# Products of 768 columns taken as two passes of 384 columns, with context and latents in one tensor

## The chip, the cores and the metric

The kernel runs on one core of a Trainium2 chip. The metric is the device time of one execution in microseconds, and the median of several runs stands for a kernel. "Columns" below are the columns of a matmul's moving operand, one per token.

## The reference, cut to what matters

Two transformer blocks run one after the other, each of two layers. The first block has 256 context tokens beside 512 latent tokens, 768 in all, and in its first layer (and in the keys and values of its second) both take part; after that only the 512 latents go on. The stretch that the change touches is this:

```python
hx = rms_norm(x, norm1_g[0]) * (1 + mod_x[1]) + mod_x[0]        # 512 latents
hc = rms_norm(s_c, norm1_g[0]) * (1 + mod_c[1]) + mod_c[0]      # 256 context tokens
y_c, y_x = hybrid_mixer(hc, hx, hyb_w_in[0], ...)               # h @ w_in, mLSTM heads, short conv, @ w_out
x = x + mod_x[2] * y_x
x = x + mod_x[5] * sqrelu_mlp(norm2(x), mlp_w1[0], mlp_w2[0])
s_c = s_c + mod_c[2] * y_c
s_c = s_c + mod_c[5] * sqrelu_mlp(norm2(s_c), mlp_w1[0], mlp_w2[0])
```

The same weights multiply the context and the latents, so one product covers 768 columns. `sqrelu_mlp` is `square(relu(h @ w1)) @ w2` with 4096 hidden channels.

## The kernel before, in words

Channels lie on the 128 partitions and tokens along the free dimension, context first (columns 0 to 255) and latents after (256 to 767). A *tile* is one weight block of 1024 by 128: it gives 128 output channels for all tokens. Weights arrive by DMA into one of four slots (`Wraw`); ScalarE writes the rounded upper part `Whi` (L1391) and VectorE the rest `Wlo` (L2038). Activations are likewise kept as a pair, `hi` and `lo`. For each of the eight 128-channel steps `k` TensorE issues three matmuls, `Whi` by `hi`, `Whi` by `lo` and `Wlo` by `hi`, each with its own weight load, all adding into the tile's accumulator. Tile `t` uses the accumulator `G[t % 2]`, two PSUM banks of 512 columns; `ps(bank, a, b)` places columns 0 to 255 in the upper half of the first bank and 256 to 767 in the whole second bank.

A product over all tokens is a FULL product; `parts(FULL)` is `[(0, 256), (256, 768)]`. The lines the text speaks of:

- `product` (L648 to L650): all eight `k` for the context columns, then all eight for the latents. So 24 matmuls of 256 columns follow each other, then 24 of 512.
- `first_products` (L675 to L677): the two first tiles of a group, interleaved over `k` because their source is still being made; three matmuls of 256 and three of 512 alternate.
- `full_part` (L827 to L829), called by `full_end` and `full_start`: the *joints*, where a layer ends with a residual and a norm and the next one begins. There the two parts are apart on purpose, since the context's norm is worked out while the latents still multiply. Two tiles end a joint and three begin the next.

The 768-column stretch is, in order: the hybrid layer's input tiles (25, the first two by another path), its output tiles (8: two by `first_products`, four by `product`, two by `full_end`), and the MLP (64 tiles in four chunks of 8 tiles up and 8 tiles down, the first three of chunk 0 by `full_start`, the last two of chunk 3 by `full_end`). The order on every engine is written out by hand, and each engine waits on semaphores.

The tensors that hold a layer's input (`h0`, `h1`) and the MLP's hidden activations (`hid0`) each come as four pieces, context and latents apart (`wide`, class `Wide`), with small spacers named `..._line` that set where a tensor begins. In the MLP, ScalarE takes a tile out of `G` with a ReLU (L1514), VectorE squares it (L2238), ScalarE writes the upper part `hid hi` in two pieces (L1518) and VectorE the rest in two pieces (L2243). In the first joint ScalarE writes the upper part of the normed input (L1473, function `upper`), VectorE the rest (L2161). Memory of finished stages is used again: the sources of the hybrid layer's output product (`mixa`, `mixb`, `mixc`) share their place with later tensors.

Of the kernel before, what the change touches and what calls it, by code (L numbers as in the profile page):

```python
# [7 lines left out]
ALU = mybir.AluOpType  # L8
# [102 lines left out]

class WideRow:
# [16 lines left out]
def build(nc, xin, cvec, wstream, adaw, firstw, vecs_d, consts_d, rope_d, poolw_d, sguw_d, rows_d, out):  # L129
    ctx = ExitStack()  # L130
    with ctx:
# [7 lines left out]
        def wide(name, ctx_line, lat_line, where, lat_first):  # L139

            half = {}
            for part, n, at in (("lat", NX, lat_line), ("ctx", NC, ctx_line))[::1 if lat_first else -1]:
                if at:
                    sb(f"{name}_{part}_line", [P, at], where=where)
                half[part] = [sb(f"{name}_{part}_{x}", [P, KD, n], F32R, where) for x in ("hi", "lo")]
            return [Wide(half["ctx"][i], half["lat"][i]) for i in range(2)]

# [81 lines left out]
        h0 = wide("h0", 16, 16, p1, False)  # L229
        p1.close()  # L230
        p2 = ExitStack()
        sb("mixa_line", [P, 112], where=p2)
# [7 lines left out]
        h1 = wide("h1", 48, 48, p4, True)  # L240
        hid0 = wide("hid0", 0, 16, p4, False)
# [95 lines left out]


# [4 lines left out]
        rep_ready, pick_ready, rstd_kept, ctx_shifted = map(sem, ("rep_ready", "pick_ready", "rstd_kept", "ctx_shifted"))  # L343
# [24 lines left out]
        chi_ready, upper_ready = map(sem, ("chi_ready", "upper_ready"))  # L368
# [22 lines left out]
        def parts(rng):  # L391
            return [(0, NC), (NC, NT)] if rng == FULL else [(NC, NT)]

# [240 lines left out]
        def _(pe):  # L634
            def product(t, src, rng, kt=KD, from_group=False):

                wait(pe, w_lo, t + 1)
                wait(pe, tile_free[t % 2], t // 2 + (-1 if from_group else 0))
                s = t % 4
                for a, b in parts(rng):  # L640
                    for k in range(kt):
                        hi, lo = src(k)
                        if is_apart(t):
                            wh, wl = [w[:, k * P:(k + 1) * P] for w in w_of(t)[1:]]
                        else:
                            wh, wl = Whi[:, s, k * P:(k + 1) * P], Wlo[:, s, k * P:(k + 1) * P]
                        o = ps(G[t % 2], a, b)
                        pe.matmul(o, wh, hi[:, a:b], start=(k == 0), stop=False)  # L648
                        pe.matmul(o, wh, lo[:, a:b], start=False, stop=False)  # L649
                        last = pe.matmul(o, wl, hi[:, a:b], start=False, stop=(k == kt - 1))  # L650
                last.then_inc(tile_done, 1)

            def first_products(t, src, rng, sem, at, kt=KD, between=None, order=None, lag=None):


                lag = lag or (3 if rng == FULL else 4)
                for n in range(kt + lag):
                    if between is not None:
                        between(n)
                    for e, nth in ((0, n), (1, n - lag)):  # L660
                        if not 0 <= nth < kt:
                            continue
                        k = order[nth] if order else nth
                        u = t + e
                        s = u % 4
                        if nth == 0:
                            wait(pe, w_lo, u + 1)
                            wait(pe, tile_free[u % 2], u // 2)
                        if e == 0:
                            pe.wait_ge(sem, (at + (nth + 1)).value())  # L670
                        hi, lo = src(k)
                        wh, wl = Whi[:, s, k * P:(k + 1) * P], Wlo[:, s, k * P:(k + 1) * P]
                        for a, b in parts(rng):
                            o = ps(G[u % 2], a, b)
# [34 lines left out]
            def first_column(i):  # L709

                pe.wait_ge(row_kept, i + 1)
                if i == 0:
                    pe.wait_ge(pick_ready, 1)
# [134 lines left out]
            def full_end(f, t0, src):  # L848

                for p in range(2):  # L850
                    for j in range(2):
# [4 lines left out]
                        for k in range(KD):  # L856
                            last = full_part(t, src, p, k, k == 0, k == KD - 1)
                            if p == 1 and j == 0 and k == 3:
                                full_stats(f, 0)
                        last.then_inc((f_a_done, tile_done)[p], 1)  # L860
# [524 lines left out]
        def _(act):  # L1385
# [74 lines left out]
            def full_edge(f, t0):  # L1460
# [41 lines left out]
            def mlp(t0, hid, rng, h0_, after, edge=None):  # L1502
# [3 lines left out]
                def chunk(i, c0, last=False):  # L1506
                    for j in range(CH):
# [4 lines left out]
                        g = e_tile(t, j) if group else ps(B6 if third else G[t % 2], a0, b0)  # L1512
# [3 lines left out]
                        for a, b in parts(rng):  # L1516
# [243 lines left out]
            for t in range(N_HYB):  # L1760
# [8 lines left out]
                g = ps(G[t % 2], a, b)  # L1769
# [256 lines left out]
        def _(dve):  # L2026
# [81 lines left out]
            def add_residual(t, m, rng, par, gate):  # L2108

                evac(t)  # L2110
                for a, b in parts(rng):
                    v = 1 if a == 0 else 0
                    last = dve.scalar_tensor_tensor(out=X[:, m, a:b], in0=ps(G[t % 2], a, b),  # L2113
# [91 lines left out]
            def mlp(t0, hid, rng, h0_, par, ada_layer, ada_par, vectors, before, after):  # L2205
# [3 lines left out]
                def chunk(i, c0, last=False):  # L2209
# [21 lines left out]
                    for j in range(CH):  # L2231
# [9 lines left out]
                        for a, b in parts(rng):  # L2241
                            hi, lo = [x.part(j, a, b) if rng == FULL else x[:, j, a - off:b - off] for x in hid]
                            last_lo = dve.tensor_tensor(lo, SQ[:, j % 2, a:b], hi.bitcast(F32), ALU.subtract)  # L2243
                        last_lo.then_inc(hid_ready, 1)
# [270 lines left out]
            for k in range(KD):  # L2515
# [3 lines left out]
                              ALU.add).then_inc(pick_ready, 1)  # L2519
# [191 lines left out]
            for t in range(N_HYB):  # L2711
                if t not in (2, 4):
                    split_lo(At(t + 2))
                g = G[t % 2]
# [23 lines left out]
                if 9 <= t < 17 and t % 2 == 0:  # L2738
# [7 lines left out]
                    dve.tensor_tensor(T[:, 0, 1:1 + NC], SQ[:, j % 2, 0:NC], ps(g, 0, NC), ALU.mult)  # L2746
                    link(dve.tensor_tensor(T[:, 0, 3 + NC:3 + NT], SQ[:, j % 2, NC:NT], ps(g, NC, NT), ALU.mult))
# [7 lines left out]
                if 17 <= t < 21:  # L2755
                    j = t - 17
                    dve.wait_ge(tile_done, t + 1)
                    dve.tensor_tensor(CY[:, j, 1:1 + NC], CY[:, j, 1:1 + NC], ps(g, 0, NC), ALU.mult)
                    link(dve.tensor_tensor(CY[:, j, 3 + NC:3 + NT], CY[:, j, 3 + NC:3 + NT], ps(g, NC, NT), ALU.mult))
# [545 lines left out]
```

## Time and profile before

| | |
|---|---|
| median of 3 runs | 2515.29 us (2514.77 to 2516.95) |
| profiled execution, first to last instruction | 2512.5 us; it is listed with no time of its own beside this span |
| TensorE busy | 2491.2 us, 99% of the span, 14058 matmuls |
| VectorE, ScalarE busy | 1611.4 us (64%), 972.5 us (39%) |
| TensorE's granted clock | mean 0.998 of full speed |
| chain that ended last | TensorE 96% |

How to read it: a row of the time line gives the start, the length, the engine, the line and the operands. Matmuls are pipelined and their ends are modelled, so the length of a matmul's row is longer than the time it costs. What a matmul costs is the distance from its start to the next one's start.

### The profile page before, as it was taken

The page shows a single profiled execution, that of the slowest core. Times are in us where ns is not written, and L with a number is a line of the kernel's source. Part 1 is how long each engine was busy: PE and PEld are TensorE (multiplying, and loading weights), DVE is VectorE, ACT ScalarE, POOL GpSimd, SP SyncE. Part 2 cuts the span into 40 slices and gives each one's busy share as a digit, 9 for nine tenths or more (in the row PEclk, how much of TensorE's full clock was granted, in tenths as well). Part 3 has the DMA queues.
Part 4 walks back from the last instruction along what each step waited for, and adds up shares of the span by engine and source line. Part 5 has one row for each costly group of instructions (what it writes and reads, how often), then busy time and mean ns, then how long its engine had stood idle before and what let it go on. Part 6 is the DMA issues. An engine that isn't in the chain of part 4 may idle for free.

```text
span 2512.5 us, 36307 instructions
## 1 busy us (share of the span) xinstructions
PE 2491.2 (99%) x14058; PEld 2125.8 (85%) x14058; DVE 1611.4 (64%) x2551; ACT 972.5 (39%) x1483; POOL 117.9 (5%) x211
## 2 busy tenths in 40 slices
PE   8999999999999999999999999999999999999998
PEld 6888888888888888779888888898888888888887
DVE  5777667665546567766655575776667777644446
ACT  6243533131313245764332244353232454533224
POOL 0000000100000000000000000010001000000000
PEclk9999999999999999999999999999999999999999
DMA  7323314433333321002545553224546323132222
GB/s 288 120 99 110 127 50 143 159 118 110 114 110 134 110 76 51 2 1 93 199 152 169 173 192 113 101 88 172 187 158 219 135 95 110 68 101 93 100 96 97
DMA packets 83965, 303.70 MB, mean 121 GB/s; under 512 B 9200, under 2 KB 11376, under 8 KB 83568
## 3 DMA queue, kind: packets, MB, share of 16 engines
q1 hardware_dynamic: 58336, 208.92, 24.0%
q0 software_dynamic: 25488, 92.81, 10.8%
q8 instruction: 100, 1.64, 0.3%
q14 instruction: 41, 0.34, 0.0%
HBM read 299.60 MB, written 2.10 MB: 120 GB/s over the span
## 4 chain that ended last, share of the span: by engine, by line
PE 96%; DMA 2%; DVE 1%; issue 0%; ACT 0%; SPq 0%; POOL 0%; POOLq 0%; ACTq 0%; DVEq 0%
PE G L648 20%; PE G L650 20%; PE G L649 20%; PE G L675 5%; PE G L676 5%; PE G L677 5%; PE G L742 2%; PE G L743 2%; PE G L744 2%; PE B L1243 2%; PE G L827 1%; DMA Araw<-adaw_dram 1%; PE G L829 1%; PE G L828 1%; PE B L1219 1%; PE G L1203 1%
## 5 line engine op out<-in xcount | busy, mean ns | idle before, releaser
L1391 ACT ACTIVATE Whi<-Wraw 128x1024 fp32r<-128x1024 f32 x333 | 349.6, 1051 | 411.4 <-DMA Wraw<-wstream_dram 399.3
L2038 DVE TENSOR_TENSOR Wlo<-Wraw,Whi 128x1024 fp32r<-128x1024 f32 x333 | 406.9, 1222 | 116.4 <-ACT Whi L1391 115.2
L648 PE MATMUL G<-hs_hi,Whi 128*128 128x512 f32 x672 | 264.2, 393 | 0.0
L650 PE MATMUL G<-hs_hi,Wlo 128*128 128x512 f32 x672 | 261.6, 389 | 0.0
L649 PE MATMUL G<-hs_lo,Whi 128*128 128x512 f32 x672 | 261.5, 389 | 0.0
L2053 DVE SCALAR_TENSOR_TENSOR Araw<-Araw,CB 128x1024 f32<-128x1024 f32 x176 | 214.3, 1220 | 20.6 <-DMA Araw<-adaw_dram 20.5
L2113 DVE SCALAR_TENSOR_TENSOR X<-G,MOD,X 128x256 f32<-128x256 f32 (+1 forms) x104 | 65.2, 655 | 206.0 <-PE G L650 154.9
L594 POOL DMA_DIRECT2D Araw<-adaw_dram x176 | 93.2, 530 | 1692.4 <-DVE Araw L2053 1637.9
L648 PE MATMUL G<-h_lat_hi,Whi 128*128 128x512 f32 x424 | 165.7, 391 | 0.0
L649 PE MATMUL G<-h_lat_lo,Whi 128*128 128x512 f32 x424 | 165.1, 389 | 0.0
L650 PE MATMUL G<-h_lat_hi,Wlo 128*128 128x512 f32 x424 | 165.1, 389 | 0.0
L648 PE MATMUL G<-hid_hi,Whi 128*128 128x512 f32 x408 | 158.9, 389 | 0.7 <-DVE X L3160 0.7
L650 PE MATMUL G<-hid_hi,Wlo 128*128 128x512 f32 x408 | 158.7, 389 | 0.0
L649 PE MATMUL G<-hid_lo,Whi 128*128 128x512 f32 x408 | 158.7, 389 | 0.0
L648 PEld LDWEIGHTS G<-hs_hi,Whi 128*128 128x128 f32 x672 | 126.2, 188 | 27.3 <-issue 1.7
L649 PEld LDWEIGHTS G<-hs_lo,Whi 128*128 128x128 f32 x672 | 126.2, 188 | 26.6 <-issue 1.0
L650 PEld LDWEIGHTS G<-hs_hi,Wlo 128*128 128x128 f32 x672 | 126.2, 188 | 26.4
L1514 ACT ACTIVATE T<-G 128x768 f32<-128x768 f32 (+1 forms) x61 | 43.0, 704 | 205.4 <-PE G L650 122.2
L2238 DVE TENSOR_TENSOR SQ<-T 128x768 f32<-128x768 f32 (+1 forms) x64 | 52.7, 823 | 87.7 <-ACT T L1514 87.7
L648 PE MATMUL G<-h_ctx_hi,Whi 128*128 128x256 f32 x368 | 104.8, 285 | 0.3 <-ACT T L1514 0.3
L649 PE MATMUL G<-h_ctx_lo,Whi 128*128 128x256 f32 x368 | 103.0, 280 | 0.0
L650 PE MATMUL G<-h_ctx_hi,Wlo 128*128 128x256 f32 x368 | 102.9, 280 | 0.0
(636 smaller groups left out, 6169.5 us busy)
## 6 DMA issues: line engine op xcount, KB each, us to landing
Wraw<-wstream_dram SPq DMA_DIRECT2D x333, 512.0 KB, 3.3
Araw<-adaw_dram POOLq DMA_DIRECT2D x176, 512.0 KB, 3.8
Eraw<-wstream_dram SPq DMA_DIRECT2D x22, 512.0 KB, 4.4
FIRST<-firstw_dram SPq DMA_DIRECT2D x6, 1024.0 KB, 18.7
X<-xin_dram SPq DMA_DIRECT2D x4, 768.0 KB, 7.0
X<-xin_dram SPq DMA_DIRECT2D x2, 1536.0 KB, 7.3
out_dram<-X SPq DMA_DIRECT2D x16, 128.0 KB, 1.7
ROW<-rows_dram SPq DMA_DIRECT2D x2, 768.0 KB, 6.5
```

The lines of the kernel that those rows point to most:

```text
L594: pool.dma_start(Araw[:, n % 2, :], adaw[bass.ds(n.value(), 1), :, :].rearrange("a p n -> p (a n)") if n.i is not None else adaw[n.c]).the ...
L648: pe.matmul(o, wh, hi[:, a:b], start=(k == 0), stop=False)
L649: pe.matmul(o, wh, lo[:, a:b], start=False, stop=False)
L650: last = pe.matmul(o, wl, hi[:, a:b], start=False, stop=(k == kt - 1))
L675: pe.matmul(o, wh, hi[:, a:b], start=(nth == 0), stop=False)
L676: pe.matmul(o, wh, lo[:, a:b], start=False, stop=False)
L677: last = pe.matmul(o, wl, hi[:, a:b], start=False, stop=(nth == kt - 1))
L1391: act.activation(hi, raw, ACT.Copy).then_inc(w_hi, 1)
L2038: dve.tensor_tensor(lo, raw, hi.bitcast(F32), ALU.subtract).then_inc(w_lo, 1)
L2053: last = dve.scalar_tensor_tensor(out=products, in0=Araw[:, n % 2, :], scalar=1.0, in1=CB[:, v, :], op0=ALU.mult, op1=ALU.mult, accum_out=o)
L2113: last = dve.scalar_tensor_tensor(out=X[:, m, a:b], in0=ps(G[t % 2], a, b), scalar=MOD[:, par, v, gate * 8 + m:gate * 8 + m + 1], in1=X[:, ...
L2238: dve.tensor_tensor(SQ[:, j % 2, a0:b0], T[:, j % 2, a0:b0], T[:, j % 2, a0:b0], ALU.mult).then_inc(hsq2_ready, 1)
```

## The change

FULL products outside the joints are taken as `(0, 384)` and `(384, 768)`. `even` says which tiles; `wide_at` places their 768 columns in the middle of the accumulator's 1024, so that each half lies in one bank.

```diff
+class Whole:
+    def part(self, k, a, b):
+        return self.ap[:, k, a:b]
...
+        def even(t):
+            c = t.c
+            if 2 <= c < T_HOUT + N_OUT - 2:
+                return True
+            return T_MLP0 + 3 <= c < T_ATT - 2
+        def wide_at(t, a, b):
+            return G[t % 2][:, P + a:P + b] if even(t) else ps(G[t % 2], a, b)
...
+        HALF = NT // 2
+        def halves(t, rng):
+            if rng == FULL and even(t):
+                return [(0, HALF), (HALF, NT)]
+            return parts(rng)
...
                 s = t % 4
-                for a, b in parts(rng):
+                for a, b in halves(t, rng):
                     for k in range(kt):
...
-                        o = ps(G[t % 2], a, b)
+                        o = wide_at(t, a, b) if rng == FULL else ps(G[t % 2], a, b)
```

A half of 384 columns crosses the border between context and latents, so the source must be one tensor. `h0`, `h1` and `hid0` become one tensor of 768 columns each (`whole`, class `Whole`); the spacer ahead of `mixa` shrinks from 112 to 32 numbers. Readers of `G` (L1514, L2113, the hybrid layer's) take `wide_at`. The hidden activations are written in one piece:

```diff
-                        for a, b in parts(rng):
-                            hi = hid[0].part(j, a, b) if rng == FULL else hid[0][:, j, a - off:b - off]
-                            last_hi = act.activation(hi, SQ[:, j % 2, a:b], ACT.Copy)
-                        last_hi.then_inc(hidhi_ready, 1)
+                        hi = hid[0].part(j, a0, b0) if rng == FULL else hid[0][:, j, a0 - off:b0 - off]
+                        act.activation(hi, SQ[:, j % 2, a0:b0], ACT.Copy).then_inc(hidhi_ready, 1)
```

The context part of the new `h1` now lies where `mixc` lay, and ScalarE writes it while the last output tile still multiplies. So that tile takes its `mixc` steps first, and ScalarE's first write waits for them (the semaphore `pick_ready` is merged into `rep_ready` to make room for `conv_used`):

```diff
-                        for k in range(KD):
-                            last = full_part(t, src, p, k, k == 0, k == KD - 1)
+                        order = HOUT_K if f == 0 and p == 1 and j == 1 else range(KD)
+                        for n, k in enumerate(order):
+                            last = full_part(t, src, p, k, n == 0, n == KD - 1)
...
+                            if f == 0 and p == 1 and j == 1 and n == 1:
+                                last.then_inc(conv_used, 1)
...
                 def upper(p, k):
+                    if f == 0 and p == 0 and k == 0:
+                        act.wait_ge(conv_used, 1)
                     act.wait_ge(f_t, 16 * f + 8 * p + k + 1)
```

On TensorE, inside the hybrid layer's input tiles, the end of one tile and the start of the next read before as follows (`h_ctx`, `h_lat` are the two pieces of the source; between the tiles stand products of the mLSTM heads):

```order
L648 MATMUL G<-h_lat_hi,Whi 128x512
L649 MATMUL G<-h_lat_lo,Whi 128x512
L650 MATMUL G<-h_lat_hi,Wlo 128x512
L1051 MATMUL B<-RM_hi,PICK 128x256
...
L648 MATMUL G<-h_ctx_hi,Whi 128x256
L649 MATMUL G<-h_ctx_lo,Whi 128x256
L650 MATMUL G<-h_ctx_hi,Wlo 128x256
```

and now:

```order
L685 MATMUL G<-h_hi,Whi 128x384
L686 MATMUL G<-h_lo,Whi 128x384
L687 MATMUL G<-h_hi,Wlo 128x384
L1091 MATMUL B<-RM_hi,PICK 128x256
...
L685 MATMUL G<-h_hi,Whi 128x384
L686 MATMUL G<-h_lo,Whi 128x384
L687 MATMUL G<-h_hi,Wlo 128x384
```

The number of matmuls and of weight loads and their places in the order stay; only the columns of each are 384 and 384 where they were 256 and 512.

On TensorE at the last tile of the first joint, second part, before:

```order
L844 MATMUL B<-CON,small 128x128
L827 MATMUL G<-mixa_hi,Whi 128x512
L828 MATMUL G<-mixa_lo,Whi 128x512
L829 MATMUL G<-mixa_hi,Wlo 128x512
```

and now, with `mixc` first:

```order
L881 MATMUL B<-CON,small 128x128
L864 MATMUL G<-mixc_hi,Whi 128x512
L865 MATMUL G<-mixc_lo,Whi 128x512
L866 MATMUL G<-mixc_hi,Wlo 128x512
L864 MATMUL G<-mixc_hi,Whi 128x512
L865 MATMUL G<-mixc_lo,Whi 128x512
L866 MATMUL G<-mixc_hi,Wlo 128x512
```

The `mixc` steps stood fourth and fifth of the tile's eight and stand first and second; the mark for ScalarE is on the sixth matmul of the tile.

On ScalarE from that joint into the MLP (with the semaphores waited for), before:

```order
L1473 ACTIVATE h_ctx_hi<-T,MOD 128x256 [waits f_t] x6
L1391 ACTIVATE Whi<-Wraw 128x1024 [waits tile_done,w_raw3]
...
L1514 ACTIVATE T<-G 128x768 [waits tile_done]
L1518 ACTIVATE hid_ctx_hi<-SQ 128x256 [waits hsq2_ready]
L1518 ACTIVATE hid_lat_hi<-SQ 128x512
L1514 ACTIVATE T<-G 128x768 [waits tile_done]
```

and now:

```order
L1515 ACTIVATE h_hi<-T,MOD 128x256 [waits f_t,conv_used]
L1515 ACTIVATE h_hi<-T,MOD 128x256 [waits f_t] x5
L1431 ACTIVATE Whi<-Wraw 128x1024 [waits tile_done,w_raw3]
...
L1557 ACTIVATE T<-G 128x768 [waits tile_done]
L1560 ACTIVATE hid_hi<-SQ 128x768 [waits hsq2_ready]
L1557 ACTIVATE T<-G 128x768 [waits tile_done]
```

The first write of the normed input has one more wait, and each hidden tile has one write where it had two; VectorE's L2243 is joined in the same way.

## Rows read from the trace of the kernel before

**Rows 1.** The page: span, busy times, TensorE's granted clock in 40 slices, the chain's shares

```profile
span 2512.5 us, 36307 instructions
...
PE 2491.2 (99%) x14058; PEld 2125.8 (85%) x14058; DVE 1611.4 (64%) x2551; ACT 972.5 (39%) x1483; POOL 117.9 (5%) x211
...
PEclk9999999999999999999999999999999999999999
...
PE 96%; DMA 2%; DVE 1%; issue 0%; ACT 0%; SPq 0%; POOL 0%; POOLq 0%; ACTq 0%; DVEq 0%
```

**Rows 2.** TensorE's waits: us in total, times, longest

```profile
PE G L751 <- DVE RS L2288: 1.5, 1, 1.5
...
PE G L648 <- ACT T L1514: 0.3, 1, 0.3
```

**Rows 3.** Time line of TensorE, MLP (start, length): 24 latent, then 24 context matmuls

```profile
410.12 0.39 PE L648 MATMUL G<-h_lat_hi,Whi 128*128 128x512 f32 x1
...
415.56 0.28 PE L648 MATMUL G<-h_ctx_hi,Whi 128*128 128x256 f32 x1
...
418.39 0.39 PE L648 MATMUL G<-h_lat_hi,Whi 128*128 128x512 f32 x1
```

**Rows 4.** Time line, a hybrid-layer tile: its second context matmul, its first latent one

```profile
245.81 0.28 PE L649 MATMUL G<-h_ctx_lo,Whi 128*128 128x256 f32 x1
...
248.42 0.39 PE L648 MATMUL G<-h_lat_hi,Whi 128*128 128x512 f32 x1
```

**Rows 5.** Time line of the context pass of rows 3, with weight loads (PEld)

```profile
415.80 0.28 PE L650 MATMUL G<-h_ctx_hi,Wlo 128*128 128x256 f32 x1
415.80 0.19 PEld L648 LDWEIGHTS G<-h_ctx_hi,Whi 128*128 128x128 f32 x1
...
415.92 0.28 PE L648 MATMUL G<-h_ctx_hi,Whi 128*128 128x256 f32 x1
```

**Rows 6.** Time line, second layer: eight matmuls of 2 columns with new weights each

```profile
964.22 0.95 PE L1161 MATMUL B<-CON,SQ 128*128 128x2 f32 x8
965.03 0.48 PE L648 MATMUL G<-h_lat_hi,Whi 128*128 128x512 f32 x1
```

**Rows 7.** TensorE by line and shape, 382 to 905 us (MLP): count, busy, mean ns

```profile
L649 PE MATMUL G<-h_lat_lo,Whi 128*128 128x512 f32 x184 | 71.6, 389 | 0.0
...
L649 PE MATMUL G<-h_ctx_lo,Whi 128*128 128x256 f32 x184 | 51.7, 281 | 0.0
...
L649 PE MATMUL G<-hid_ctx_lo,Whi 128*128 128x256 f32 x176 | 49.5, 281 | 0.0
...
L676 PE MATMUL G<-hid_ctx_lo,Whi 128*128 128x256 f32 x64 | 18.0, 281 | 0.0
...
L676 PE MATMUL G<-h_ctx_lo,Whi 128*128 128x256 f32 x48 | 13.5, 281 | 0.0
```

**Rows 8.** The same, 49 to 286.5 us (hybrid layer, input tiles)

```profile
L649 PE MATMUL G<-h_ctx_lo,Whi 128*128 128x256 f32 x184 | 51.3, 279 | 0.0
```

**Rows 9.** The same, 286.5 to 345 us (hybrid layer, output tiles): one latent, one context group

```profile
L648 PE MATMUL G<-mixa_hi,Whi 128*128 128x512 f32 x16 | 6.3, 395 | 0.0
...
L649 PE MATMUL G<-mixa_lo,Whi 128*128 128x256 f32 x16 | 4.5, 280 | 0.0
```

**Rows 10.** Time line, first joint: a matmul of the last output tile, ScalarE's first write

```profile
350.58 0.39 PE L829 MATMUL G<-mixa_hi,Wlo 128*128 128x512 f32 x1
...
351.75 0.91 ACT L1473 ACTIVATE h_ctx_hi<-T,MOD 128x256 fp32r<-128x256 f32 x2 [1.15 <-DVE T L2154]
```

**Rows 11.** Time line, start of the MLP: ScalarE writes a hidden tile, takes the next out

```profile
380.71 0.42 ACT L1518 ACTIVATE hid_ctx_hi<-SQ 128x256 fp32r<-128x256 f32 x1 [1.03 <-DVE SQ L2238]
381.03 0.61 ACT L1518 ACTIVATE hid_lat_hi<-SQ 128x512 fp32r<-128x512 f32 x1
381.55 0.79 ACT L1514 ACTIVATE T<-G 128x768 f32<-128x768 f32 x1
```

More of the change, by code:

```diff
@@ L109, in row, with __init__ @@
         return WideRow(self, k)
+class Whole:
+    def __init__(self, ap):
+        self.ap = ap
+    def part(self, k, a, b):
+        return self.ap[:, k, a:b]
+    def row(self, k):
+        return WideRow(self, k)
 class WideRow:
@@ L146, in wide, with whole @@
             return [Wide(half["ctx"][i], half["lat"][i]) for i in range(2)]
+        def whole(name, at, where):
+            if at:
+                sb(f"{name}_line", [P, at], where=where)
+            return [Whole(sb(f"{name}_{x}", [P, KD, NT], F32R, where)) for x in ("hi", "lo")]
         def sem(name):
@@ L228, in build @@
         p1 = ExitStack()
-        h0 = wide("h0", 16, 16, p1, False)
+        h0 = whole("h0", 32, p1)
         p1.close()
         p2 = ExitStack()
-        sb("mixa_line", [P, 112], where=p2)
+        sb("mixa_line", [P, 32], where=p2)
         mixa = [sb("mixa_hi", [P, 4, NT], F32R, p2), sb("mixa_lo", [P, 4, NT], F32R, p2)]
@@ L239, in build @@
         p4 = ExitStack()
-        h1 = wide("h1", 48, 48, p4, True)
-        hid0 = wide("hid0", 0, 16, p4, False)
+        h1 = whole("h1", 48, p4)
+        hid0 = whole("hid0", 128, p4)
         p4.close()
@@ L672, in first_products @@
                         wh, wl = Whi[:, s, k * P:(k + 1) * P], Wlo[:, s, k * P:(k + 1) * P]
-                        for a, b in parts(rng):
-                            o = ps(G[u % 2], a, b)
+                        for a, b in halves(u, rng):
+                            o = wide_at(u, a, b) if rng == FULL else ps(G[u % 2], a, b)
                             pe.matmul(o, wh, hi[:, a:b], start=(nth == 0), stop=False)
@@ L855, in full_end @@
                             wait(pe, tile_free[t % 2], t // 2)
-                        for k in range(KD):
-                            last = full_part(t, src, p, k, k == 0, k == KD - 1)
-                            if p == 1 and j == 0 and k == 3:
+                        order = HOUT_K if f == 0 and p == 1 and j == 1 else range(KD)
+                        for n, k in enumerate(order):
+                            last = full_part(t, src, p, k, n == 0, n == KD - 1)
+                            if p == 1 and j == 0 and n == 3:
                                 full_stats(f, 0)
+                            if f == 0 and p == 1 and j == 1 and n == 1:
+                                last.then_inc(conv_used, 1)
                         last.then_inc((f_a_done, tile_done)[p], 1)
@@ L1511, in chunk @@
                         third = rng == FULL and c0 == 0 and j == 2
-                        g = e_tile(t, j) if group else ps(B6 if third else G[t % 2], a0, b0)
+                        g = e_tile(t, j) if group else ps(B6, a0, b0) if third else \
+                            wide_at(t, a0, b0) if rng == FULL else ps(G[t % 2], a0, b0)
                         evac(t, split=not (c0 == 0 and j < (2 if rng == FULL else 4)))
@@ L1768, in _ @@
                 evac(At(t))
-                g = ps(G[t % 2], a, b)
+                g = wide_at(At(t), a, b)
                 if t == 0:
@@ L2112, in add_residual @@
                     v = 1 if a == 0 else 0
-                    last = dve.scalar_tensor_tensor(out=X[:, m, a:b], in0=ps(G[t % 2], a, b),
+                    last = dve.scalar_tensor_tensor(out=X[:, m, a:b],
+                                                    in0=wide_at(t, a, b) if rng == FULL else ps(G[t % 2], a, b),
                                                     scalar=MOD[:, par, v, gate * 8 + m:gate * 8 + m + 1],
@@ L2240, in chunk @@
                         wait(dve, hidhi_ready, hn + 1)
[L2241 to L2244, printed above, removed]
+                        hi, lo = [x.part(j, a0, b0) if rng == FULL else x[:, j, a0 - off:b0 - off] for x in hid]
+                        dve.tensor_tensor(lo, SQ[:, j % 2, a0:b0], hi.bitcast(F32), ALU.subtract).then_inc(hid_ready, 1)
                     if last and rng == FULL:
@@ L2713, in _ @@
                     split_lo(At(t + 2))
-                g = G[t % 2]
                 if t in (1, 3):
```

18 lines of the change are left out of this document (9 added, 9 removed).

## The prediction

> **What bounds the kernel now.** I read the page first. TensorE is busy for 99% of a span of 2512.5 us, its clock is at the full level (2.4 GHz) in every slice, and the chain that ended last is 96% TensorE [rows 1]. The waits come next: outside the start, where the input arrives, TensorE's longest wait is 1.5 us, and in the stretch of the change it waits once, for 0.3 us [rows 2]. So no other engine, no transfer and no clock sets the time there. Only a lower price of the matmuls themselves can shorten this kernel, and the third view to read is the time line of TensorE, start to start.
>
> In the MLP, 24 latent matmuls of 512 columns begin at 410.12 and the first context matmul at 415.56 us: 5.44 / 24 = 226.7 ns each. The 24 context matmuls of 256 columns end their turn at 418.39: 2.83 / 24 = 117.9 ns each [rows 3]. Half the columns should cost 113.3, so each context matmul pays 4.6 ns that the latent ones don't. In the hybrid layer there are tiles without it: 23 context matmuls from 245.81 to 248.42 us take 2.61 / 23 = 113.5 ns [rows 4]. The price by the column is therefore the same at 256 as at 512 columns, 0.443 ns, with no fixed part left over, and 117.9 is something else that ends later.
>
> The time line with the weight loads names it. The load for the next matmul begins when the matmul before it begins (both at 415.80), and the next matmul begins 0.12 us later [rows 5]. How short that step can get is seen where columns cost nothing: eight matmuls of two columns, each with new weights, take 965.03 - 964.22 = 0.81 us, or 101 ns each [rows 6]. A change of weights thus costs 0.10 us or more whatever the columns; 113 is just above that, and a small disturbance makes the weights the later of the two. At 226.7 they are ready long before. At 384 columns the stream is 0.443 x 384 = 170.0 ns, 52 ns above the 117.9 of a slow weight change.
>
> **The change, part by part.**
>
> *The halves.* Every changed step of three matmuls keeps its number of matmuls and loads. A pair costs 226.7 + 117.9 = 344.6 ns before where it is slow, 340.0 where it is not, and 2 x 170.0 = 340.0 after.
> - MLP: per line 184 + 176 + 64 + 48 = 472 context matmuls, three lines, 1416 pairs. All groups have a mean length of 281 ns [rows 7], which is that of the slow tiles, so nearly all are slow; one tile of 24 behind the wait in rows 2 runs at the other price. 1392 x 4.6 ns = 6.4 us.
> - Hybrid layer, input tiles: 184 x 3 = 552 pairs. The mean length is 279 instead of 281 [rows 8]; a tile without the extra would show 276 or 277, so about half are slow. 276 x 4.6 ns = 1.3 us.
> - Hybrid layer, output tiles (two by `first_products`, four by `product`): 6 x 8 x 3 = 144 pairs, mean 280 [rows 9], counted as slow: 0.7 us.
>
> All of it lies on the path, since TensorE is the path.
>
> *The place of `mixa` and `mixb`.* Their latent matmuls have means up to 395 ns where all others have 389 [rows 7, 9]. The change moves both tensors. The trace doesn't show what makes them dearer, so the gain lies between 0 and, at up to 6 ns for one of the three lines and half of that as a mean, 144 x 3 ns = 0.4 us. I take 0.3, nearer the upper end, because `mixa` and `mixb` alone differ and the new place starts like that of the other tensors.
>
> *The new wait in the first joint.* ScalarE's first write of the normed input now waits for the last tile's sixth matmul. That place in the tile begins at 350.58 and its row ends at 350.97; ScalarE began the write at 351.75, held by VectorE [rows 10]. The wait is over 0.8 us before. It costs nothing; what hides it is VectorE's chain ahead of the write. Queued behind it on ScalarE would be the other seven context writes and a weight's upper part, and TensorE's next tile needs the first of them. The order of that tile's eight steps moves nothing else: its sources are all long there.
>
> *The hidden tile in one write.* ScalarE's two writes fill 381.55 - 380.71 = 0.84 us; one of 768 columns should cost about what the ReLU of the same size does, 0.79 [rows 11]. VectorE's pair shrinks alike. This is hidden behind TensorE in all 32 cases but the first, where TensorE's 0.3 us wait ends with the ReLU behind these writes [rows 2, 11]. Bounds 0 and 0.3 us; I take 0.1. Reading `G` across the border of two banks adds no instruction, and sits beside TensorE's work.
>
> *A rule against it.* The trace gives one price by the column, 0.443 ns, at 256 and at 512 columns [rows 3, 4]. The Trainium skill (TensorE: Matmul & The Clock Gate, Back-to-back issue gap) gives a single matmul's gap as N / 2.4 + 2.5 ns; two of 384 are then 325.0 ns and so are 256 and 512, and the whole gain is nil. The same page (LDWEIGHTS) puts a load at 128 / 1.2 = 107 ns, less than any matmul here, so no context matmul would be held by it. Neither gives the 117.9 nor the 226.7 of the rows, so my sum goes by the rows.
>
> **The sum.** 6.4 + 1.3 + 0.7 + 0.3 + 0.1 = 8.8 us. The profiled span of 2512.5 would become 2503.7. The page gives no time around the span; the median of the runs, 2515.29, stands 2.8 us above it, and nothing outside the span changes. So 2515.3 - 8.8 = 2506.5 us, 0.35% faster. A measurement of this kernel can tell about 0.2%, 5 us, from no change.
>
> **The rivals.**
>
> *A. A fixed cost by matmul, no gain.* If the two distances of rows 3 are a fixed part and a part by the column, the part by the column is (226.7 - 117.9) / 256 = 0.425 ns and the fixed one 9.1; 384 columns cost 172.3 and a pair 344.6, as before. The slow pairs gain nothing, the 300 fast ones lose 4.6 each, 1.4 us, and the small terms give 0.4 back: 2516.3 us. The skill's gap rule above is of this form. For it: two sizes alone are measured. Against it: the tiles at 113.5 ns, which such a price can't reach. 11%.
>
> *B. Whole pieces, slower.* At 2.4 GHz 256 columns are 106.7 ns; a matmul of 256 costs 6.6 more and one of 512 twice that. If this extra comes by begun pieces of 256 columns, 384 columns pay two of them: 160.0 + 13.3 = 173.3 ns, and a pair is 346.6. Against the forecast that adds 6.6 ns to each of 2112 pairs, 14.0 us: 2520.5 us, 0.2% slower. It fits all rows, since none has a size between; but nothing else in the trace counts in pieces of 256. It decides from 8.8 us / 4224 = 2.1 ns on: above 172.1 ns for a matmul of 384 the kernel is slower than before. 5%.
>
> *C. The change doesn't do all it says.* The halves could still be held now and then, through reads of the longer tensors or the evacuations; at 171 ns instead of 170 the gain falls by 4.2 us, to 2510.7. 5%.
>
> **How the numbers follow.** The forecast has 79%. Its own range is 2504 to 2510: the terms can be off by 1 us each way, and medians of this kernel differ by a microsecond or two. The range of 2503.5 to 2511 takes in C too and leaves out A and B, 16%. Faster by over 0.2% needs less than 2510.3: the forecast and part of C, 0.82. Within 0.2%: A and the rest of C, 0.13. Slower: most of B, 0.05.
>
> **What would show it.** In the changed profile matmuls of 128x384 stand 170.0 ns apart, 24 in 4.08 us, through both halves of a tile and at the same price in the hybrid layer and the MLP. TensorE's waits in the first joint stay under 0.5 us, and ScalarE's first write there still follows VectorE. 172 ns or more between starts, a ScalarE wait for TensorE at that write, or a gain that falls outside 40 to 905 us would make the prediction wrong.

## The result and the profile after

The changed kernel takes 2520.45 us (median of 13 runs, 2518.69 to 2522.57), the kernel before 2514.77 in the same number of runs beside it. The ratio is 1.0024, with a 95% interval of 1.0017 to 1.0031: slower by 5.7 us, where 8.8 us were to be gained. The time is that of rival B, 2520.5.

The page of the changed kernel, against [rows 1]: span, busy times and the chain's shares.

```profile
span 2518.7 us, 36244 instructions
...
PE 2499.4 (99%) x14058; PEld 2217.3 (88%) x14058; DVE 1611.8 (64%) x2519; ACT 969.8 (39%) x1451; POOL 117.9 (5%) x211
...
PE 97%; DMA 1%; DVE 1%; ACT 1%; SPq 0%; issue 0%; ACTq 0%; DVEq 0%
```

The span grew by 6.2 us and TensorE's busy time by 8.2, with the same 14058 matmuls. ScalarE and VectorE have 32 instructions fewer each, the joined hidden writes, and about the same busy time. So the time is in TensorE. Its waits say whether it stood still (to be read like [rows 2]):

```profile
PE G L685 <- DVE Wlo L2079: 0.3, 1, 0.3
PE G L685 <- ACT T L1557: 0.2, 1, 0.2
```

It did not. The wait of 0.3 us falls at 1211.56 us, where only latents go on; in the stretch of the change TensorE waits once, for 0.2 us. What is left is the price of the matmuls. The time line of TensorE in the MLP (start, length; to be read start to start, like [rows 3]):

```profile
410.04 0.33 PE L685 MATMUL G<-h_hi,Whi 128*128 128x384 f32 x1
...
418.36 0.33 PE L685 MATMUL G<-h_hi,Whi 128*128 128x384 f32 x1
```

From 410.04 to 418.36 us there are 48 matmuls, both halves of a tile: 8.32 / 48 = 173.3 ns each, where 170.0 were forecast. A pair costs 346.7 ns; before it cost 226.7 + 117.8 = 344.5. The price is the same in every group of the MLP; two lines by shape there, of `product` and of `first_products`, to be compared with [rows 7]:

```profile
L686 PE MATMUL G<-h_lo,Whi 128*128 128x384 f32 x368 | 122.9, 334 | 0.0
...
L713 PE MATMUL G<-h_lo,Whi 128*128 128x384 f32 x96 | 32.1, 334 | 0.0
```

Where it falls by stage, in us, from the starts of the stages' first matmuls in the two profiled executions (for instance the MLP from 386.56 to 877.51 us now, 382.49 to 870.23 before):

| stretch | before | after | difference |
|---|---|---|---|
| hybrid layer, input tiles | 237.09 | 240.82 | +3.7 |
| its output tiles | 50.91 | 50.85 | -0.1 |
| first joint | 45.12 | 45.26 | +0.1 |
| MLP products | 487.74 | 490.96 | +3.2 |
| second joint | 55.07 | 55.19 | +0.1 |
| latents alone, to the last large products | 1578.78 | 1577.98 | -0.8 |

The MLP's 3.2 us are the new price: 1416 pairs by 346.7 - 344.5 = 2.2 ns make 3.1. Of the hybrid layer's 3.7 us, 1.5 are not the change's (the last section shows this); a kernel with the unchanged code and the same disturbance takes 238.61, so the change costs 2.2 us there. The last line of the table isn't touched by the change. TensorE's waits of over 0.1 us in it sum to 5.7 us before and 5.2 now, which is 0.5 of its 0.8 us; the rest stays unexplained.

### The profile page after: what moved, and what is told of

Read it like the earlier page. It is cut to its first block, busy times and chain, and to the rows that moved or that the text cites. A ratio compares the mean times of both kernels' runs of the same rounds, so it can differ in the third digit from the quotient of the medians.

```text
span 2518.7 us, 36244 instructions
## 1 busy us (share of the span) xinstructions
PE 2499.4 (99%) x14058; PEld 2217.3 (88%) x14058; DVE 1611.8 (64%) x2519; ACT 969.8 (39%) x1451; POOL 117.9 (5%) x211
## 4 chain that ended last, share of the span: by engine, by line
PE 97%; DMA 1%; DVE 1%; ACT 1%; SPq 0%; issue 0%; ACTq 0%; DVEq 0%
PE G L685 21%; PE G L687 21%; PE G L686 20%; PE G L712 5%; PE G L714 5%; PE G L713 5%; PE G L779 2%; PE G L780 2%; PE G L781 2%; PE B L1283 2%; PE G L864 1%; PE G L866 1%; PE G L865 1%; PE B L1259 1%; PE G L1243 1%; PE G L1259 1%
## 5 line engine op out<-in xcount | busy, mean ns | idle before, releaser
L2079 DVE TENSOR_TENSOR Wlo<-Wraw,Whi 128x1024 fp32r<-128x1024 f32 x333 | 406.9, 1222 | 117.5 <-ACT Whi L1431 116.4
L685 PE MATMUL G<-h_hi,Whi 128*128 128x384 f32 (+1 forms) x896 | 310.8, 347 | 0.4 <-DVE Wlo L2079 0.3
L687 PE MATMUL G<-h_hi,Wlo 128*128 128x384 f32 (+1 forms) x896 | 308.9, 345 | 0.0
L686 PE MATMUL G<-h_lo,Whi 128*128 128x384 f32 (+1 forms) x896 | 308.9, 345 | 0.0
L686 PE MATMUL G<-hid_lo,Whi 128*128 128x512 f32 (+1 forms) x760 | 276.3, 364 | 0.0
L687 PE MATMUL G<-hid_hi,Wlo 128*128 128x512 f32 (+1 forms) x760 | 276.3, 364 | 0.0
L685 PE MATMUL G<-hid_hi,Whi 128*128 128x512 f32 (+1 forms) x760 | 276.3, 364 | 0.0
L685 PEld LDWEIGHTS G<-h_hi,Whi 128*128 128x128 f32 x896 | 168.7, 188 | 9.6 <-issue 2.7
L687 PEld LDWEIGHTS G<-h_hi,Wlo 128*128 128x128 f32 x896 | 168.7, 188 | 6.3
L686 PEld LDWEIGHTS G<-h_lo,Whi 128*128 128x128 f32 x896 | 168.6, 188 | 6.3
L687 PEld LDWEIGHTS G<-hid_hi,Wlo 128*128 128x128 f32 x760 | 142.7, 188 | 15.9
```

Source lines behind the costliest of these rows:

```text
L2079: dve.tensor_tensor(lo, raw, hi.bitcast(F32), ALU.subtract).then_inc(w_lo, 1)
```

## The experiments

### The passes of 256 and 512 columns, on the joined tensors

The changed kernel with the halves alone undone: the tensors, the one-piece hidden write and the joint stay as changed.

```diff
         def even(t):
-            c = t.c
-            if 2 <= c < T_HOUT + N_OUT - 2:
-                return True
-            return T_MLP0 + 3 <= c < T_ATT - 2
+            return False
```

> The changed kernel with its passes put back to 256 and 512 columns; the joined tensors, the moved mixa, the single hidden write and the new wait stay. Theory P (a matmul pays 6.7 ns for each begun piece of 256 columns, so 384 costs 173.3): the loss is all in the halves, so this one is at 2514.3 us (2514.8 less up to 0.8 for the small terms), ratio 0.9998. Theory F (each matmul that follows a new weight load pays a fixed 13.3 ns): the same time, if the 256-column passes still stand 117.9 ns apart; 2519 if they now pay the full 13.3 and stand 120.0 apart everywhere. Theory D (the 384-column passes are dear because of where the joined tensors or the shifted accumulator lie, not because of their size): 2514.3 if the accumulator is to blame, above 2517 if the joined tensors are.

Measured: 2523.21 us, ratio to the kernel before 1.0033 (1.0021 to 1.0045). It is slower than the changed kernel by 2.8 us, and not equal to the kernel before, as theories P and F had it; of the three only D, for the joined tensors, allowed for more than 2517. TensorE's time line in the MLP: the first context matmul of a tile, the first three latent ones, and the next tile's first.

```profile
411.98 0.28 PE L682 MATMUL G<-h_hi,Whi 128*128 128x256 f32 x1
...
414.85 0.40 PE L682 MATMUL G<-h_hi,Whi 128*128 128x512 f32 x1
...
415.32 0.39 PE L684 MATMUL G<-h_hi,Wlo 128*128 128x512 f32 x1
...
420.31 0.28 PE L682 MATMUL G<-h_hi,Whi 128*128 128x256 f32 x1
```

24 context matmuls take 2.87 us, 119.6 ns each with the one that leads in and 120 within, not 117.8. The first three latent matmuls stand (415.32 - 414.85) / 2 = 235 ns apart; later ones come back to 226.7. So the two parts of the change do different things: with all of the change but the halves, the joined tensors where they now lie among it, the kernel is about 8.5 us slower, and the halves took 2.8 us of that back.

### Matmuls of many sizes, by themselves

The kernel before, and behind its output rows of 32 equal matmuls, each with new weights and a small mark of 64 columns (L1388) ahead of each row. The rows add work, so only the distances of the rows count, not the total (2762.56 us).

```diff
+            for n in (512, 480, 448, 416, 384, 352, 320, 288, 272, 256, 240, 224, 192, 128):
+                row_of(n)
+            for off in (16, 32, 48, 64):
+                row_of(256, off=off)
...
+            for n in (512, 384, 256, 192, 128):
+                row_of(n, m=64)
+            for n in (512, 384, 256, 192, 128):
+                row_of(n, m=32)
+            row_of(256, at=128)
+            row_of(384, at=128)
...
```

> The kernel before with some 1400 matmuls added after the end of its last output, on tensors that lie still; the output is untouched and the time grows by 250 to 300 us. Rows of 32 equal matmuls with a new weight load each, and what one costs, start to start. Theory P (6.7 ns for each begun piece of 256 columns): 480, 448, 416, 352, 320, 288, 272 columns cost 213.3, 200.0, 186.7, 160.0, 146.7, 133.3, 126.7 ns; 256 columns 113.3 where the load allows it; with 64 or 32 weight columns, whose loads are short, 512 stays 226.7, 384 173.3, 256 113.3. Theory F (13.3 ns by matmul and weight load): the same down to 272, but 256 columns 120.0, and with 64 or 32 weight columns the extra shrinks: 512 at 220 and 217, 384 at 167 and 163. Theory D (a place, not a size; 0.443 ns a column): 212.5, 198.3, 184.2, 155.8, 141.7, 127.5, 120.4 ns for the sizes above, and 384 columns 170.0 at offsets where they lie well; the rows that start 16 to 64 numbers further, or at another place of the bank, differ from each other.

The time line of its rows, from within each row (start, length of the group, count) to the next row's mark:

```profile
2556.82 4.32 PE L1391 MATMUL G<-hs_hi,Whi 128*128 128x384 f32 x24
2560.99 0.19 PE L1388 MATMUL B<-hs_hi,Whi 128*128 128x64 f32 x1
...
2562.21 4.16 PE L1391 MATMUL G<-hs_hi,Whi 128*128 128x352 f32 x25
2566.21 0.20 PE L1388 MATMUL B<-hs_hi,Whi 128*128 128x64 f32 x1
...
2580.78 2.80 PE L1391 MATMUL G<-hs_hi,Whi 128*128 128x256 f32 x22
2583.42 0.20 PE L1388 MATMUL B<-hs_hi,Whi 128*128 128x64 f32 x1
...
2591.78 2.84 PE L1391 MATMUL G<-hs_hi,Whi 128*128 128x192 f32 x24
2594.47 0.22 PE L1388 MATMUL B<-hs_hi,Whi 128*128 128x64 f32 x1
...
2607.73 2.20 PE L1391 MATMUL G<-hs_hi,Whi 128*128 128x256 f32 x18
2609.77 0.19 PE L1388 MATMUL B<-hs_hi,Whi 128*128 128x64 f32 x1
```

384 columns: (2560.99 - 2556.82) / 24 = 173.8 ns. 352: 4.00 / 25 = 160.0. 256: 2.64 / 22 = 120.0, and with the operand begun 48 numbers further 2.04 / 18 = 113.3 (the last two lines). 192: 2.69 / 24 = 112.1, and about the same at 224 and at 128 columns: in these rows the weight change sets the price, whatever the columns.

At 2.4 GHz 384 columns are 160.0 ns, 352 are 146.7, 320 are 133.3. All three measure 13.3 ns more, as 512 does (213.3 and 226.7). 256 columns (106.7) pay 6.7 at the best place. So a fixed extra for every size is out, and so is the forecast's price by the column: 0.443 x 384 is 3.3 ns short. The sizes between 384 and 512 don't fit 13.3 at this place: 416, 448 and 480 columns take 188.3, 206.6 and 216.7 ns, which is 15.0, 20.0 and 16.7 over. The accumulator is not to blame: 384 columns written 128 columns further into the bank, where the changed kernel's first half goes, take 173.3 as well.

With 64 or 32 weight columns instead of 128 the weight change costs less, and the extra shows without it:

```profile
2679.45 3.83 PE L1391 MATMUL G<-hs_hi,Whi 128*64 128x256 f32 x32
2683.11 0.20 PE L1388 MATMUL B<-hs_hi,Whi 128*128 128x64 f32 x1
...
2702.28 2.75 PE L1391 MATMUL G<-hs_hi,Whi 128*32 128x256 f32 x22
2704.87 0.19 PE L1388 MATMUL B<-hs_hi,Whi 128*128 128x64 f32 x1
...
2708.81 1.06 PE L1391 MATMUL G<-hs_hi,Whi 128*32 128x128 f32 x15
2709.71 0.24 PE L1388 MATMUL B<-hs_hi,Whi 128*128 128x64 f32 x1
```

With 32 weight columns 128 columns are down to 0.90 / 15 = 60 ns, and with 64 they are too, but 256 with 32 still take 2.59 / 22 = 117.7. With 64 they take 3.66 / 32 = 114.4 with the one that leads in and 113.3 within; 48 numbers further into the operand it is 119.0 (the rows of the run on sizes around 256). A weight change that fits into 60 ns cannot be what holds 256 columns at 117.7 or 119.0. So the prediction's reading of [rows 5, 6], weights that come late, isn't needed for such a price. That the weights have no part in it isn't shown: at one place of the operand 128, 64 and 32 weight columns give 120.0, 113.3 and 117.7.

### The context tensors moved by 64 bytes, nothing else

The kernel before, with the spacers alone altered. Of the tensors that multiply, only the context's move.

```diff
-        h0 = wide("h0", 16, 16, p1, False)
+        h0 = wide("h0", 32, 0, p1, False)
...
-        h1 = wide("h1", 48, 48, p4, True)
-        hid0 = wide("hid0", 0, 16, p4, False)
+        h1 = wide("h1", 64, 48, p4, True)
+        hid0 = wide("hid0", 0, 0, p4, False)
```

> The kernel before, passes of 256 and 512 as they were and tensors apart; only the three context tensors begin 64 bytes further, where the joined tensors begin too (counted modulo 256 bytes), and the latents stay where they were. Theory W (what a pass of 256 columns costs hangs on where its moving operand begins: in the rows of equal matmuls 120.0 ns there, 117.8 ns 64 bytes further): the context passes go from 117.8 to 120.0 ns in the MLP and from about 116 to 120 in the hybrid layer, 1416 x 2.2 + 552 x 4.3 = 5.5 us, so 2520 us, ratio 1.0022. Theory J (the undone halves were slow because one joined tensor is read, not because of where it begins): no change, 2514.6 us.

Measured: 2523.26 us, ratio 1.0031 (1.0019 to 1.0042), within 0.1 us of the joined tensors with 256 and 512. The same places of its time line, and a line by shape from the tiles where passes of 256 and 512 alternate:

```profile
412.10 0.28 PE L648 MATMUL G<-h_ctx_hi,Whi 128*128 128x256 f32 x1
...
414.97 0.40 PE L648 MATMUL G<-h_lat_hi,Whi 128*128 128x512 f32 x1
...
415.44 0.39 PE L650 MATMUL G<-h_lat_hi,Wlo 128*128 128x512 f32 x1
```

```profile
L675 PE MATMUL G<-hid_lat_hi,Whi 128*128 128x512 f32 x64 | 25.5, 398 | 0.0
```

In the passes of 24 the context matmuls stand at 120.0 ns, and the latent ones, whose tensors lie as before, start up at 235 ns. Where the two sizes alternate it is the latent ones that got dearer: mean lengths up to 398 where they had 389, and start to start 232.2 ns where they had 226.7. So what costs 8 us is where the context's moving operand begins, and not that the tensors are joined: the MLP takes 492.98 us here and in the run with the joined tensors. The 3 us beyond the expectation are on the 512 columns behind the context's, 1.9 us of them in the MLP's tiles where the sizes alternate.

### The place, step by step

Again rows of matmuls behind the kernel's output, now in the kernel's own pattern: 24 of 512 columns, then 24 of 256 that begin a number of 32-byte steps further each time.

```diff
+            for off in range(0, 128, 8):
+                mark()
+                steps(512, 0, 0)
+                steps(256, off, off)
```

> The kernel before with a thousand matmuls added after its output, in the real pattern (upper by upper, upper by lower, lower by upper): 24 of 512 columns, then 24 of 256 that begin 0 to 480 bytes further in steps of 32, then the same with the two operands at different places, then 24 of 384 in steps of 32 bytes. Theory W: the 256-column rows fall into groups by place, 120.0 ns at a multiple of 128 bytes from the tensor's start, 117.8 or 113.3 at 64 bytes from it; the 384-column rows lie between 173.2 and 176 at all places and never near 170, so no place would have saved the halves. Theory R (256 columns cost 113.3 or 117.8 by what ran before, not by place): behind the 24 of 512 every 256-column row stands at 117.8 or 120, none at 113.3.

```profile
2534.03 0.28 PE L1391 MATMUL G<-hs_hi,Whi 128*128 128x256 f32 x1
...
2536.91 0.20 PE L1388 MATMUL B<-hs_hi,Whi 128*128 128x64 f32 x1
...
2542.49 0.28 PE L1391 MATMUL G<-hs_hi,Whi 128*128 128x256 f32 x1
...
2545.29 0.19 PE L1388 MATMUL B<-hs_hi,Whi 128*128 128x64 f32 x1
```

The first place costs 2.88 / 24 = 120.0 ns, the next 2.80 / 24 = 116.7. Eight places give 120.0, 116.7, 117.9, 120.1, 119.8, 118.9, 117.8 and 118.3, and then repeat: the period is 256 bytes. Behind passes of 512 none is near 113.3. At 384 columns the price within a pass lies between 173.1 and 176.7, at no place near 170.

### Two places tried in the kernels

The changed kernel with its joined tensors 64 bytes further:

```diff
-        h0 = whole("h0", 32, p1)
+        h0 = whole("h0", 48, p1)
...
-        h1 = whole("h1", 48, p4)
+        h1 = whole("h1", 64, p4)
```

> The changed kernel with its joined tensors begun 64 bytes further, so that both halves begin where the context tensors did before the change (counted modulo 256 bytes). Theory S (a pass of 384 columns costs 173.3 for its size, nearly wherever it begins; rows of 384 in the real pattern gave 173.1 there): no change against the changed kernel, 2520.4 us, passes 173.1 to 173.4 ns apart. Theory Q (the halves could stand at 170.0 in another place, and it was the place that failed the change): 2506 to 2512 us.

Measured: 2519.23 us, ratio to the kernel before 1.0018 (1.0009 to 1.0028). Its time line, 24 matmuls apart:

```profile
410.12 0.34 PE L685 MATMUL G<-h_hi,Whi 128*128 128x384 f32 x1
...
414.28 0.34 PE L685 MATMUL G<-h_hi,Whi 128*128 128x384 f32 x1
```

4.16 / 24 = 173.3 ns. The halves cost the same at both places, and the rows above have no place near 170: their price does not come from where they lie.

The kernel before, with the context at the cheapest of the eight places (116.7), and `mixa` and `mixb` moved as in the change:

```diff
-        h0 = wide("h0", 16, 16, p1, False)
+        h0 = wide("h0", 40, 56, p1, False)
...
-        sb("mixa_line", [P, 112], where=p2)
+        sb("mixa_line", [P, 32], where=p2)
...
-        h1 = wide("h1", 48, 48, p4, True)
-        hid0 = wide("hid0", 0, 16, p4, False)
+        h1 = wide("h1", 72, 48, p4, True)
+        hid0 = wide("hid0", 0, 56, p4, False)
```

> The kernel before, passes of 256 and 512 and tensors apart, with the context tensors begun 96 bytes further (the place where the rows of the real pattern were cheapest, 116.7 ns) and mixa and mixb moved as in the change. Theory W (place sets the price of the 256-column passes): 116.7 for 117.8 in the MLP, 1416 x 1.1 = 1.5 us, and 0.3 us for mixa; 2513 us, unless the 512-column passes behind start up slower, as the rows of that place hint (227.2 for 226.7), which would take 0.7 back. Without W: no change, 2514.8.

Measured: 2519.08 us, ratio 1.0015 (1.0006 to 1.0024): slower, where 2513 was expected. Its time line, and a line by shape of the MLP, of the kernel before and of this one:

```profile
411.03 0.28 PE L648 MATMUL G<-h_ctx_hi,Whi 128*128 128x256 f32 x1
...
413.83 0.39 PE L648 MATMUL G<-h_lat_hi,Whi 128*128 128x512 f32 x1
...
414.30 0.39 PE L650 MATMUL G<-h_lat_hi,Wlo 128*128 128x512 f32 x1
```

```profile
L676 PE MATMUL G<-hid_lat_lo,Whi 128*128 128x512 f32 x64 | 24.9, 389 | 0.0
```

```profile
L676 PE MATMUL G<-hid_lat_lo,Whi 128*128 128x512 f32 x64 | 25.6, 400 | 0.0
```

The context pass is as cheap as expected, 2.80 / 24 = 116.7 ns. The latent matmuls behind it pay that back: 235 ns at the start of the pass, 227.7 in the mean. Where the two sizes alternate the latent ones cost more than that, mean lengths up to 400 and 234.3 ns start to start for 226.7. On the MLP's 336 of them that is 2.6 us, and the MLP is 2.5 us longer. A place can't be priced by the pass that reads there alone.

The run shows one thing more. The hybrid layer's output tiles, which read `mixa` and `mixb`, take 51.15 us (from 289.73 to 340.88), and 51.15 in the run without the halves too, where both tensors lie at the same new place. Before it was 50.91, and it is 50.91 where only the context moved. So moving these two tensors cost 0.24 us.

### Sizes around 256 and 384, with three weight widths

Rows behind the output once more, all begun 48 numbers on.

```diff
+            for m in (32, 64):
+                for n in (128, 160, 192, 224, 240, 256, 264, 272, 288, 320, 352, 384, 400, 416, 448, 480, 496, 512):
+                    row_of(n, m=m, off=48)
+            for n in (240, 248, 256, 264, 272, 288, 320, 352, 384, 400, 416, 448, 480, 496, 512):
+                row_of(n, off=48)
```

> The kernel before with rows of 32 equal matmuls after its output, 128 to 512 columns, with 32, 64 and 128 weight columns, all begun at the place where 256 columns cost 113.3. Theory P (6.7 ns on top of the columns at 2.4 GHz for each begun piece of 256): at 32 and 64 weight columns 128, 192, 240, 256 columns cost 60.0, 86.7, 106.7, 113.3, and from 264 on the extra is 13.3: 123.3, 126.7, 133.3, 146.7, 173.3, 226.7; the step stands between 256 and 264. Theory F (13.3 ns by matmul, with short loads less): one extra at all sizes for one weight width. Theory L (a price by the column, 0.443 ns): a straight line, 116.9 at 264, 141.7 at 320, 170.0 at 384.

```profile
2708.32 2.77 PE L1391 MATMUL G<-hs_hi,Whi 128*128 128x256 f32 x23
2710.93 0.19 PE L1388 MATMUL B<-hs_hi,Whi 128*128 128x64 f32 x1
...
2711.78 3.29 PE L1391 MATMUL G<-hs_hi,Whi 128*128 128x264 f32 x26
2714.91 0.19 PE L1388 MATMUL B<-hs_hi,Whi 128*128 128x64 f32 x1
...
2734.75 4.58 PE L1391 MATMUL G<-hs_hi,Whi 128*128 128x384 f32 x25
2739.16 0.19 PE L1388 MATMUL B<-hs_hi,Whi 128*128 128x64 f32 x1
```

256 columns: 2.61 / 23 = 113.5 ns, 6.8 over their columns. 264: 3.13 / 26 = 120.4, 10.4 over. 320, not shown, take 146.7, 13.4 over. 384: 4.41 / 25 = 176.4 at this place, 16.4 over. Eight columns past 256 cost 7 ns where their own time is 3.3. Over all rows of these two runs, with 128, 64 and 32 weight columns, the cheapest that a size was seen at is 6.7 over its columns for 256, and about 13.3 for 320, 352, 384, 416, 448, 480 and 512. Whole pieces of 256 thus give the lowest price of these sizes, but there is no clean step between: 264, 272 and 288 columns pay 10.0, 10.2 and 11.1 at their cheapest and not 13.3. At this one place 256 pays 6.8 with 128 weight columns, 12.3 with 64 and 10.0 with 32. The extra depends on size, place and weight width, and its law stays open.

### The context pass in another order

In the tiles at 113.5 ns [rows 4] a context matmul reaches the price by the column; behind passes of 512 it costs 117.8. One difference between the kernel and the rows of equal matmuls is that `hi` and `lo` alternate. The kernel before, with each context pass of `product` ordered by term:

```diff
+                    if b == NC:
+                        o = ps(G[t % 2], a, b)
+                        for term in range(3):
+                            for k in range(kt):
...
+                        continue
```

> The kernel before; in the tiles taken by product alone the 24 context matmuls stand in another order: first the eight steps of upper by upper, then the eight of upper by lower, then the eight of lower by upper. Same matmuls, same tensors and places, same 512-column passes. Theory T (a context matmul stands at 117.8 or at 113.3 by how the reads of its weights and of its moving operand fall together from one matmul to the next; a row of equal matmuls on one operand stayed at 113.3): the passes fall to 113.3, 1080 x 4.5 ns in the MLP and some 1.5 us in the hybrid layer, 2508 to 2509 us, ratio 0.9975. Theory W alone (place is all): no change, 2514.7.

Measured: 2514.46 us, ratio 0.9999 (0.9990 to 1.0008). Two passes of its time line, one behind TensorE's wait at the start of the MLP, one in its middle:

```profile
386.57 1.07 PE L647 MATMUL G<-h_ctx_lo,Whi 128*128 128x256 f32 x8
387.47 0.39 PE L647 MATMUL G<-h_ctx_hi,Wlo 128*128 128x256 f32 x2
...
410.37 1.10 PE L647 MATMUL G<-h_ctx_hi,Whi 128*128 128x256 f32 x8
...
413.19 0.39 PE L657 MATMUL G<-h_lat_hi,Whi 128*128 128x512 f32 x1
```

(413.19 - 410.37) / 24 = 117.5 ns behind 512 columns, 0.90 / 8 = 112.5 behind the wait. The order isn't it. In the kernels the low price was seen only in passes behind an interruption (a wait, or other products), but not behind each. Of the 19 context passes of the hybrid layer behind other products, in the kernel before, 12 stand within the pass at 113.3 to 114.3 ns and 7 at 117.7 to 117.8. All five behind the products of L1079 are among the 7, all four behind those of L1052 among the 12. And the MLP's first pass, behind the same wait of 0.3 us, stands at 114.0 in the kernel before and at 117.8 in the three runs with rows behind the output. Why, no run settled. No kernel of this study clearly beat the kernel before.

## Why the prediction was wrong

**The step that failed** is this one: "The price by the column is therefore the same at 256 as at 512 columns, 0.443 ns, with no fixed part left over". Two points, 113.5 and 226.7 ns, lie on a line through zero, and the prediction drew it. They lie as well on "columns at 2.4 GHz plus 6.7 up to 256, plus 13.3 at 512", which rival B had written down, and nothing in the trace had a size between. 384 columns cost 160.0 + 13.3 = 173.3 ns, not 170.0. B got 5% on the ground that nothing else in the trace counts in pieces of 256, which is no evidence about a price that the trace doesn't show. B's number came true. Its rule holds for the cheapest rows of 256 and of 320 to 512 columns, and not for the sizes just past 256; that the change used only sizes that it fits is in part luck. Why a matmul of 384 columns pays 13.3 ns stays open.

**The size of the error is that step, to about a microsecond.** 2 x 3.33 ns by 2112 pairs is 14.1 us; 2506.5 + 14.1 = 2520.6, measured 2520.45. That it fits to 0.2 us is luck too: medians of this kernel differ by a microsecond or two, and the two profiled spans, less the disturbance of 1.5 us, differ by 4.7 us where the new price asks for 14.1 - 8.8 = 5.3. By stage:
- MLP: forecast -6.4. With 346.7 for a pair it is +3.0, measured +3.2.
- Hybrid input tiles: forecast -1.3. With the new price +2.4, measured +2.2 against unchanged code with the same disturbance. The fast tiles of [rows 8] lose most, as rival A had said of them.
- Output tiles: forecast -0.7 for the pairs and -0.3 for the place of `mixa` and `mixb`, measured -0.1. The term for the place had the wrong sign: with passes of 256 and 512 the move costs 0.24 us, and the halves took 0.30 back. The pairs there had not cost 344.6 as counted but 117.8 + 229.2 = 347.0, in the four tiles by `product`; the halves stand at 174.2.

**What was right.** TensorE is the path, and the count of pairs holds. The slow context passes are gone: outside the stretch of the disturbance the halves cost 173 to 175 ns within a pass, in both stages. The new wait in the first joint costs nothing; the changed kernel's time line there, TensorE's sixth matmul of the tile and ScalarE's first write (compare [rows 10]):

```profile
354.64 0.39 PE L866 MATMUL G<-mixc_hi,Wlo 128*128 128x512 f32 x1
...
355.87 0.91 ACT L1515 ACTIVATE h_hi<-T,MOD 128x256 fp32r<-128x256 f32 x2 [1.21 <-DVE T L2196]
```

ScalarE is still held by VectorE, and the matmul's row ends 0.84 us before the write begins. The hidden tile in one write gave the 0.1 us: TensorE's wait for ScalarE at the MLP's start fell from 0.3 to 0.2.

**The explanation of 117.9.** Late weights are not needed for it: 256 columns cost 117.7, and at another place 119.0, where weights change in 60 ns or less, and with 128 weight columns the price of the context pass moves from 116.7 to 120.1 with the place of the operand alone. It moves with what ran before as well. What makes it stays open.

**The rule that was weighed.** The Trainium skill (TensorE: Matmul & The Clock Gate, Back-to-back issue gap) gives a single matmul's gap as N / 2.4 + 2.5 ns, which makes an estimate of 162.5 ns for 384 columns. The trace disagrees: 173.3, and the extra over the columns is 6.7 to 20 ns, not 2.5. Its consequence, no gain in a pair, was nearer than the forecast.

## What to carry to other kernels

Two sizes that share a price by the column don't give the price of a third: where a change trades two known sizes for an unknown one, and the gain is a few ns on thousands of matmuls, the unknown price deserves an even chance for each law that fits the known points. And a change that moves an operand moves its price: shifting the context's tensors by 64 bytes cost 8 us here, more than the 2.8 us that the change of size gave on the joined tensors, so the two are to be tried apart. The pass behind has to be read as well as the pass that moved.

## What the runs showed of the hardware

- **Extra by size.** A matmul with new weights costs its columns at 2.4 GHz plus 6.7 ns for 256 at the best place, and plus 13.3 at the best place for the sizes measured from 320 to 512; elsewhere up to 20.0 over (448 columns, 206.6 ns). With 128 weight columns the rows of 128, 192 and 224 columns all take about 112 ns, and eight matmuls of 2 columns took 101 each [rows 6]; with 32 or 64 weight columns, 128 columns take 60.
- **The operand's place.** 256 columns cost 116.7 to 120.1 ns in the kernel's pattern, by where the moving operand begins within 256 bytes, and the passes of 512 behind them start at 227 ns in the kernel before and at 235 ns in the kernels with the context moved.
- **The clock.** In the changed kernel's profile TensorE's granted clock falls to half its full level, 1.2 GHz, for 3.4 us from 85.9 us on. Stretches of 1 us (busy times, then the granted clock), of the changed kernel and then of the kernel with rows of sizes, which has the unchanged code there:

```profile
85.00:86.00 1.00, 1.00 (x9) 0.98 (x9) 0.00 (x0) 0.24 (x1) 0.00 (x0) 0.95 0.98 352
86.00:87.00 1.00, 1.00 (x5) 1.00 (x4) 0.00 (x0) 0.98 (x3) 0.00 (x0) 0.50 0.94 344
```

```profile
86.00:87.00 1.00, 1.00 (x7) 1.00 (x6) 0.00 (x0) 1.00 (x1) 0.00 (x0) 0.50 1.02 389
```

Ahead of it TensorE runs nearly 2 us of matmuls of 6 columns (L1044 in the changed kernel), its rows unbroken. Half the clock for 3.4 us costs about 1.7 us, by an estimate; the hybrid layer's input tiles are 1.5 us longer with it in unchanged code. The profiled execution of the kernel before has the same matmuls and no such fall, all others of this study have it, the one of the reordered context pass for 6.8 us. So it is no effect of the change, but 1.5 us or so of the 6.2 that the two spans differ by. How often it falls in the other executions can't be seen: of them only the mean clock is on record, 0.996 to 0.999 of full speed, and every profile has another fall at its end.
